# Eleven reciprocal square roots: from Ln and Exp on ScalarE to Sqrt on ScalarE and a reciprocal on VectorE

## The chip, the core and the metric

One core of a Trainium2 chip runs the whole program. The metric is the device time of one execution in microseconds (us), as the median of several runs. TensorE (PE) does the matrix products, ScalarE (ACT) the activation functions, VectorE (DVE) elementwise work, GpSimd (POOL) a few side jobs, and SyncE (SP) issues the loads.

## The reference, cut to what matters

Two transformer-like blocks run one behind the other on 512 positions of width 1024. In between and inside them stand RMS norms. Each of them needs, for every position, the reciprocal square root of a mean of squares over the features:

```python
def rms_norm(x, w):
    y = xf * lax.rsqrt(jnp.mean(xf * xf, axis=-1, keepdims=True) + EPS)
    return (y * w.astype(jnp.float32)).astype(x.dtype)

def _rmsnorm(x, g):
    y = x32 * lax.rsqrt(jnp.mean(x32 * x32, axis=-1, keepdims=True) + RMS_EPS)
    return y.astype(x.dtype) * g
```

Eleven such norms run over whole activations: at the start of the first block (528 positions, 16 meta tokens among them), ahead of its feed-forward part, at its end, ahead of and behind each of the second block's two feed-forward parts and its attention part, and for the two low-rank projections (256 and 768 features). The head norms inside the attention branches are computed by other code.

## The kernel before, in words

Activations lie transposed: features on the 128 partitions, positions in the free dimension. A norm goes like this. ScalarE squares the chunks of 128 features one by one, and VectorE adds them up into one tile (`ssq` or `ss2`). TensorE multiplies that tile with a matrix of ones (`sum_squares`, L687), so that each partition of the PSUM tile `A[0]` holds the sum for every position. ScalarE then makes the reciprocal root in SBUF (`rstd` or `rs2`) in its helper `root`: a Ln with scale 1/features and bias eps (L1219), a drain, and an Exp with scale -0.5 (L1221), which releases the semaphore `nrm_root`. VectorE waits for it in its helper `rooted`, and then multiplies the activations by the root: in `scaled` (lines L1754, L1995, L2082, L2249, L2271), in the final norm of the first block (L2069), or in `residual` (L2089, L2093), which adds the normed output to the stream. In `scaled` the product passes to ScalarE, which makes its high part (`hi_part`, L1227; with `modulate`, L1434, in between in the second block), and VectorE takes the low part (L1714). TensorE multiplies only when a chunk has both parts.

The root is as wide as the positions of its norm: 528 once, 768 four times (512 positions and 256 of context), and 512 six times. All eleven use all 128 partitions.

Every weight tile goes a similar way: SP loads it (`raw`), ScalarE makes the high part (`w_hi`, L1190), VectorE the low part (`w_lo`, L1676), and TensorE multiplies three times (`unit`, L675). Two slots are used in turn. Every engine runs its instructions in the written order; order between engines comes from counting semaphores only. ACTIVATE instructions need their function's table on ScalarE; where it isn't there, the compiler puts an ACT_TABLE_LOAD ahead, which the source doesn't show. Other functions in the program are Exp (attention, L1305, L1525, L1587), Silu (L1257, L1452), Sigmoid (L1270, L1620), Relu, Square, Copy and Identity.

Of the kernel before, what the change touches and what calls it, by code (L numbers as in the profile page):

```python
# [26 lines left out]
ACT = mybir.ActivationFunctionType  # L27
# [5 lines left out]
SEQ = 512  # L33
META = 16
T1 = META + SEQ
CTX = 256
T2 = CTX + SEQ
# [171 lines left out]
def build(nc, I, out):  # L209
    with ExitStack() as ctx:  # L210
        def sem(name):
            return ctx.enter_context(nc.semaphore(name))

        def ps(name, cols):
            return ctx.enter_context(nc.psum_tensor(name, [P, cols], F32))
# [3 lines left out]
        def at(name, off, shape, dt=F32):  # L219
            return nc.alloc_sbuf_tensor_at(name, [P] + list(shape), dt, offset=base0 + off)  # L220
# [25 lines left out]
        def cst(name, lo=0, hi=P):  # L246
            a, n = _C[name]
            return const[lo:hi, a:a + n]
# [3 lines left out]
        eps_col = cst("eps")  # L252
# [14 lines left out]
        rstd = at("rstd", SCR + 5 * 4 * T1, [T1])  # L267
# [75 lines left out]
        rs2 = at("rstd2", E + 3 * 4 * T2, [T2])  # L343
# [57 lines left out]
        A = [ps(f"aux{s}", 1024) for s in range(2)]  # L401
# [26 lines left out]
        nrm_root = sem("nrm_root")  # L428
# [33 lines left out]
        def two(ap, n):  # L462

            return ap.rearrange("p (s n) -> p s n", s=2)

        def acc(t, geo, rows=P, lo=0):

            n = geo[0][1]
            if len(geo) == 1:
                return t[lo:rows, 0:n]  # L470
            return t[:, :].rearrange("p (s n) -> p s n", s=2)[lo:rows, :, 0:n]

        def like(ap, geo):

            return ap if len(geo) == 1 else two(ap, geo[0][1])
# [704 lines left out]
        def _(act):  # L1180
# [30 lines left out]
            def root(dst, geo, features):  # L1211

                nroot[0] += 1
                act.drain()
                act.wait_ge(nrm_sum, nroot[0])
                n0 = geo[0][0]
                n1 = geo[-1][0] + geo[-1][1]
                v = dst[:, n0:n1]
                act.activation(like(v, geo), acc(A[0], geo), ACT.Ln, bias=eps_col, scale=1.0 / features)  # L1219
                act.drain()  # L1220
                act.activation(v, v, ACT.Exp, scale=-0.5).then_inc(nrm_root, 1)  # L1221

            def hi_part(dst, src):

# [12 lines left out]
            for c in range(KC):  # L1237
                act.wait_ge(xT_out, c + 1)
                square(X[:, c, :], sqb, T1)
            root(rstd, G1, D)  # L1240
            for c in range(KC):
                hi_part(HH[:, c, :], tmp[c % 2][:, :])


            with act.Fori(0, RET_H) as h:
                u = Count(U_RET, (h, 6))
                for k, dst in enumerate((rq, rk, rvT[0], rvT[1])):
                    done(u + k)
                    geo = G1 if k else GM
# [115 lines left out]
            with act.Fori(0, KC // 2) as i:  # L1365
                for e in range(2):
                    u = Count(U_CONV + 3 * e, (i, 6))
                    for k, dst in enumerate((cb, cc)):
                        s = (u + k).slot
                        done(u + k)  # L1370
                        geo = G1 if k else GM
# [8 lines left out]
            for n in range(KC):  # L1380
                u = Count(U_OUT + n)
                split(u + 2)
                act.wait_ge(evicted[u.slot], val(u.turns() + 2))
                square(X[:, n, META:T1], sqb, SEQ)
            root(rstd, GS, D)
            for c in range(KC):
                hi_part(HH[:, c, META:T1], tmp[c % 2][:, 0:SEQ])
# [20 lines left out]
            with act.Fori(0, 4) as i:  # L1408
                for e in range(2):
# [3 lines left out]
                    square_in_turn(X[:, bass.ds(i * 2 + e, 1), META:T1], sqb, SEQ, i, e)  # L1413
            nsq[0] += KC
            root(rstd, GS, D)


# [196 lines left out]
            with act.Fori(0, KC) as n:  # L1614
                u = Count(U_GATE, (n, 4))
                for k in range(2):
                    v = u + 2 * k
# [3 lines left out]
                                   bias=col_b[:, bass.ds(n + (48 + KC * k), 1)]).then_inc(evicted[v.slot], 1)  # L1621
# [49 lines left out]
        def _(dve):  # L1671
# [13 lines left out]
            def add_square(dst, buf, n, first):  # L1685

                b = buf[nsq[0] % 2][:, 0:n]
                nsq[0] += 1
                dve.drain()
                dve.wait_ge(nrm_sq, nsq[0])  # L1690
                if first:
                    dve.tensor_copy(dst, b).then_inc(nrm_add, 1)
                else:
                    dve.tensor_tensor(dst, dst, b, ALU.add).then_inc(nrm_add, 1)  # L1694
# [4 lines left out]
                dve.wait_ge(nrm_sq, val(turn(i, nsq[0] + 1 + e, 2)))  # L1699
                dve.tensor_tensor(dst, dst, buf[(nsq[0] + e) % 2][:, 0:n], ALU.add).then_inc(nrm_add, 1)  # L1700

            def rooted():

                nroot[0] += 1
                dve.drain()
                dve.wait_ge(nrm_root, nroot[0])

            def scaled(chunks, bufs, hi, lo, scale):

                n0 = nap[0]  # L1710

                def low(c):
                    dve.wait_ge(ap_hi, n0 + c + 1)
                    dve.tensor_tensor(lo(c), bufs(c), hi(c).bitcast(F32), ALU.subtract).then_inc(ap_lo, 1)  # L1714

                for c in range(chunks):
                    if c >= 2:
                        dve.drain()
                    scale(c, bufs(c)).then_inc(ap_tmp, 1)
                    if c >= 1:  # L1720
                        low(c - 1)
                low(chunks - 1)
                nap[0] += chunks
                dve.drain()
# [19 lines left out]
            for c in range(KC):  # L1744
# [3 lines left out]
                if c >= 1:  # L1748
                    add_square(ssq[:, :], sqb, T1, c == 1)
            add_square(ssq[:, :], sqb, T1, False)  # L1750
            rooted()

            scaled(KC, lambda c: tmp[c % 2][:, :], lambda c: HH[:, c, :], lambda c: HL[:, c, :],
                   lambda c, b: dve.scalar_tensor_tensor(out=b, in0=X[:, c, :], scalar=col_a[:, c:c + 1],  # L1754
# [229 lines left out]
            for n in range(KC):  # L1984
# [5 lines left out]
                if n >= 1:  # L1990
                    add_square(ssq[:, 0:SEQ], sqb, SEQ, n == 1)
            add_square(ssq[:, 0:SEQ], sqb, SEQ, False)
            rooted()
            scaled(KC, lambda c: tmp[c % 2][:, 0:SEQ], lambda c: HH[:, c, META:T1], lambda c: HL[:, c, META:T1],
                   lambda c, b: dve.scalar_tensor_tensor(out=b, in0=X[:, c, META:T1], scalar=col_a[:, 8 + c:9 + c],  # L1995
                                                         in1=rstd[:, 0:SEQ], op0=ALU.mult, op1=ALU.mult))
# [62 lines left out]
            dve.memset(ssq[:, 0:SEQ], 0.0)  # L2059
            ff_down(FF1 // D - 1, True)  # L2060
            nsq[0] += KC
            rooted()


            def by_column(ap):
# [8 lines left out]
            def sums2(n0):  # L2074
                for c in range(KC):
                    add_square(ss2[:, n0:T2], tm2, T2 - n0, c == 0)
                rooted()

            def normed(n0):

# [3 lines left out]
            def residual(i, n0):  # L2084

                for c in range(KC):
                    for e, (a, b) in enumerate(((CTX, T2), (0, CTX))):
                        if a >= n0:
                            dve.scalar_tensor_tensor(out=Y2[:, c, a:b], in0=Y2[:, c, a:b], scalar=resg[i][:, c, e:e + 1],  # L2089
                                                     in1=rs2[:, a:b], op0=ALU.mult, op1=ALU.mult)  # L2090
                    dve.drain()  # L2091
                    x = X2[:, c, n0:T2]
                    dve.tensor_tensor(x, x, Y2[:, c, n0:T2], ALU.add).then_inc(x2_out, 1)  # L2093

            sums2(0)
            normed(0)

# [51 lines left out]
            dve.wait_ge(rpb_in, 16 * GRID_H)  # L2149
            dve.wait_ge(y_zero, 1)  # L2150
            swiglu(U_FA, G2, 0, 32, False, True)
            rooted()
            residual(0, 0)
            sums2(0)
            normed(0)

# [87 lines left out]

            for k in range(2):
                add_square(ss2[:, :], tm2, T2, k == 0)
            rooted()
            scaled(2, lambda c: tm2[c % 2][:, :], lambda c: CKH[:, c, :], lambda c: CKL[:, c, :],
                   lambda c, b: dve.scalar_tensor_tensor(out=b, in0=ckvT[:, c, :], scalar=col_b[:, 70 + c:71 + c],  # L2249
                                                         in1=rs2[:, :], op0=ALU.mult, op1=ALU.mult))  # L2250
# [15 lines left out]
            rotate(mkr[R, CTX:T2], 1)  # L2266
            dve.drain()
            dve.tensor_copy(mks[0][R, :], mkr[R, :])
            rooted()
            scaled(6, lambda c: tm2[c % 2][:, 0:SEQ], lambda c: CQH[:, c, :], lambda c: CQL[:, c, :],  # L2270
                   lambda c, b: dve.scalar_tensor_tensor(out=b, in0=cqT[:, c, :], scalar=col_b[:, 64 + c:65 + c],  # L2271
                                                         in1=rs2[:, 0:SEQ], op0=ALU.mult, op1=ALU.mult))
# [67 lines left out]
            with dve.Fori(0, KC) as n:  # L2340
                u = Count(U_GATE, (n, 4))
                for k in range(2):
                    v = u + (2 * k)
# [18 lines left out]
                    split(Count(U_OUT2 + 2 + e, (i, 2)))  # L2362
                    add_in_turn(ss2[:, CTX:T2], tm2, SEQ, i, e)
            nsq[0] += KC
            rooted()
            residual(1, CTX)
            sums2(CTX)
            normed(CTX)
            dve.wait_ge(y_zero, 2)
            swiglu(U_FB, GL, CTX, 54, True, False)  # L2370
            rooted()
            residual(2, CTX)


# [32 lines left out]
```

## Time and profile before

| | |
|---|---|
| median of 3 runs | 3187.33 us (3177.83 to 3195.09) |
| profiled execution, its own time | 3191.74 us |
| span of the profile | 3190.0 us |
| TensorE / VectorE / ScalarE busy | 91% / 46% / 34% of the span |
| mean granted clock of TensorE | 0.947 of full speed |
| ACT_TABLE_LOAD at the eleven roots | 22, two for each |

Busy time is the time in which an engine executes something. Idle time of an engine matters only where TensorE in the end waits for it too.

### The profile page before, as it was taken

The page shows a single profiled execution, that of the slowest core. Times are in us where ns is not written, and L with a number is a line of the kernel's source. Part 1 is how long each engine was busy: PE and PEld are TensorE (multiplying, and loading weights), DVE is VectorE, ACT ScalarE, POOL GpSimd, SP SyncE. Part 2 cuts the span into 40 slices and gives each one's busy share as a digit, 9 for nine tenths or more (in the row PEclk, how much of TensorE's full clock was granted, in tenths as well). Part 3 has the DMA queues.
Part 4 walks back from the last instruction along what each step waited for, and adds up shares of the span by engine and source line. Part 5 has one row for each costly group of instructions (what it writes and reads, how often), then busy time and mean ns, then how long its engine had stood idle before and what let it go on. Part 6 is the DMA issues. An engine that isn't in the chain of part 4 may idle for free.

```text
span 3190.0 us, 42398 instructions
## 1 busy us (share of the span) xinstructions
PE 2903.6 (91%) x14689; PEld 2441.5 (77%) x14689; DVE 1461.0 (46%) x2270; ACT 1083.0 (34%) x1597; POOL 35.4 (1%) x27
## 2 busy tenths in 40 slices
PE   6999999899998999959999998499888899599997
PEld 4778777689876888749999998488656677378885
DVE  4335444445655666563333324654444334533335
ACT  3223455432223223253222123432433344442322
POOL 0000000000000000010000000000000000000000
PEclk9999999899999999979999999699989899799998
DMA  3224211234433555322222222001100023123332
GB/s 105 60 65 139 67 46 53 62 123 123 126 116 108 161 164 158 113 58 59 66 59 66 63 61 61 20 27 32 44 17 14 22 70 95 52 86 95 95 92 66
DMA packets 423953, 248.13 MB, mean 78 GB/s; under 512 B 15289, under 2 KB 403850, under 8 KB 423738
## 3 DMA queue, kind: packets, MB, share of 16 engines
q1 hardware_dynamic: 423866, 247.01, 26.4%
q8 instruction: 50, 0.82, 0.1%
q14 instruction: 37, 0.30, 0.0%
HBM read 244.88 MB, written 2.10 MB: 77 GB/s over the span
## 4 chain that ended last, share of the span: by engine, by line
PE 69%; issue 20%; DVE 5%; ACT 4%; DVEq 1%; ACTq 1%; DMA 0%; POOL 0%; POOLq 0%
PE unit_acc L675 62%; PE aux L1081 2%; PE aux L1105 2%; PE aux L660 1%; PE aux L994 1%; ACT w_hi L1190 1%; DVE ssq L1694 1%; PE aux L687 1%; DVE x L2093 1%; DVE mla_stat L2294 1%; ACT h_hi L1227 1%; DVE w_lo L1676 1%; PE aux L976 1%; PE aux L760 1%; DVEq L2091 0%
## 5 line engine op out<-in xcount | busy, mean ns | idle before, releaser
L675 PE MATMUL unit_acc<-h_hi,w_hi 128*128 128x512 f32 (+2 forms) x2816 | 885.5, 360 | 60.9 <-DVE h_lo L1714 39.5
L675 PE MATMUL unit_acc<-h_lo,w_hi 128*128 128x512 f32 (+2 forms) x2816 | 866.6, 354 | 0.0
L675 PE MATMUL unit_acc<-h_hi,w_lo 128*128 128x512 f32 (+2 forms) x2816 | 864.9, 353 | 0.0
L1676 DVE TENSOR_TENSOR w_lo<-raw,w_hi 128x1024 fp32r<-128x1024 f32 (+3 forms) x405 | 484.8, 1197 | 620.2 <-ACT w_hi L1190 619.3
L1190 ACT ACTIVATE w_hi<-raw 128x1024 fp32r<-128x1024 f32 (+3 forms) x405 | 419.7, 1036 | 841.2 <-PE unit_acc L675 787.0
L675 PEld LDWEIGHTS unit_acc<-h_hi,w_hi 128*128 128x128 f32 x2816 | 504.7, 191 | 153.9 <-issue 50.6
L675 PEld LDWEIGHTS unit_acc<-h_hi,w_lo 128*128 128x128 f32 x2816 | 507.3, 191 | 57.6
L675 PEld LDWEIGHTS unit_acc<-h_lo,w_hi 128*128 128x128 f32 x2816 | 508.9, 191 | 53.0
L675 PE MATMUL unit_acc<-branch_hi,w_hi 128*128 128x512 f32 x448 | 178.3, 398 | 0.0
L675 PE MATMUL unit_acc<-branch_lo,w_hi 128*128 128x512 f32 x448 | 177.5, 396 | 0.0
L675 PE MATMUL unit_acc<-branch_hi,w_lo 128*128 128x512 f32 x448 | 177.4, 396 | 0.0
L675 PE MATMUL unit_acc<-u_hi,w_hi 128*128 128x384 f32 (+1 forms) x528 | 159.2, 356 | 0.0
L675 PE MATMUL unit_acc<-u_hi,w_lo 128*128 128x384 f32 (+1 forms) x528 | 159.1, 355 | 0.0
L675 PE MATMUL unit_acc<-u_lo,w_hi 128*128 128x384 f32 (+1 forms) x528 | 159.1, 355 | 0.0
L1819 DVE SCALAR_TENSOR_TENSOR ada_sum<-ada_raw,silu_c,ada_sum 128x512 f32<-128x512 f32 x203 | 145.8, 749 | 18.6 <-issue 13.4
L2119 DVE TENSOR_TENSOR y<-unit_acc,y 128x768 f32 (+2 forms) x48 | 39.6, 825 | 175.4 <-PE unit_acc L675 175.4
L2104 DVE TENSOR_TENSOR tmp<-unit_acc,tmp 128x768 f32<-128x768 f32 (+1 forms) x44 | 36.3, 825 | 167.1 <-PE unit_acc L675 167.1
L687 PE MATMUL aux<-ssq,const 128*128 128x384 f32 (+2 forms) x32 | 22.2, 820 | 97.1 <-DVE ssq L1694 83.8
L675 PEld LDWEIGHTS unit_acc<-u_hi,w_hi 128*128 128x128 f32 x528 | 96.4, 188 | 8.3 <-DVE u_lo L2110 0.3
L675 PEld LDWEIGHTS unit_acc<-u_hi,w_lo 128*128 128x128 f32 x528 | 96.4, 188 | 8.1
L675 PEld LDWEIGHTS unit_acc<-u_lo,w_hi 128*128 128x128 f32 x528 | 96.4, 188 | 8.0
L675 PEld LDWEIGHTS unit_acc<-branch_hi,w_lo 128*128 128x128 f32 x448 | 84.3, 188 | 20.7
(282 smaller groups left out, 2989.0 us busy)
## 6 DMA issues: line engine op xcount, KB each, us to landing
raw<-in_w_in_dram SPq DMA_DIRECT2D x132, 512.0 KB, 3.9
raw<-in_ffn_w_dram SPq DMA_DIRECT2D x120, 512.0 KB, 3.8
ada_raw<-in_w_ada_dram SPq DMA_DIRECT2D x72, 512.0 KB, 4.7
raw<-in_w_up_dram SPq DMA_DIRECT2D x32, 512.0 KB, 4.3
raw<-in_w_down_dram SPq DMA_DIRECT2D x32, 512.0 KB, 3.9
raw<-in_w_branch_dram SPq DMA_DIRECT2D x24, 512.0 KB, 3.9
raw<-in_w_out_dram SPq DMA_DIRECT2D x16, 512.0 KB, 3.8
raw<-in_ffn_w_dram SPq DMA_DIRECT2D x16, 384.0 KB, 3.4
```

The lines of the kernel that those rows point to most:

```text
L660: return pe.transpose(dst, src, ident[k0:k0 + k, k0:k0 + k])
L675: last = pe.matmul(G[s][0:n, 512 * j:512 * j + m], w[s][:, k, 0:n], x[:, k, a:a + m], start=(k == 0 and i == 0), stop=(k == kc - 1 and i = ...
L687: last = pe.matmul(A[0][:, 512 * j:512 * j + m], ones, src[:, a:a + m], start=True, stop=True)
L760: last = pe.matmul(A[1][:, a:a + 1], s[:, c * P:c * P + P], ones[:, 0:1], start=True, stop=True)
L976: pe.matmul(A[0][:, b:b + 256], q, nk[r, a:a + 256], start=True, stop=True)
L1081: last = pe.matmul(A[0][:, a:a + m], mq[0:QK, P * t:P * t + P], mk[0:QK, a:a + m], start=True, stop=True)
L1105: last = pe.matmul(A[1][:, 768:768 + VD], mT[t % 2][:, j, :], mV[:, j, :], start=(j == 0), stop=(j == 5))
L1190: act.activation(wh[v.slot][:, 0:kc, :], raw[v.slot][:, 0:kc, :], ACT.Copy).then_inc(hi_split, 1)
L1676: dve.tensor_tensor(wl[s][:, 0:kc, :], raw[s][:, 0:kc, :], wh[s][:, 0:kc, :].bitcast(F32), ALU.subtract).then_inc(lo_split, 1)
L1819: last = dve.scalar_tensor_tensor(out=s[:, :], in0=w, scalar=c, in1=s[:, :], op0=ALU.mult, op1=ALU.add)
L2104: dve.tensor_tensor(like(tm2[1][:, n0:T2], geo), acc(G[s], geo), like(tm2[0][:, n0:T2], geo), ALU.mult).then_inc(evicted[s], 1)
L2119: dve.tensor_tensor(y, p, y, ALU.add).then_inc(evicted[u.slot], 1)
```

## The change

`root` makes a Sqrt in place of Ln, drain and Exp, and releases the semaphore from it. `rooted` is given the tile and its columns, takes the reciprocal of it in place on VectorE after the wait, and drains. All eleven callers of `rooted` pass the tile on.

```diff
@@ ScalarE, root(dst, geo, features)
-                act.activation(like(v, geo), acc(A[0], geo), ACT.Ln, bias=eps_col, scale=1.0 / features)
-                act.drain()
-                act.activation(v, v, ACT.Exp, scale=-0.5).then_inc(nrm_root, 1)
+                act.activation(like(v, geo), acc(A[0], geo), ACT.Sqrt, bias=eps_col,
+                               scale=1.0 / features).then_inc(nrm_root, 1)
@@ VectorE
-            def rooted():
+            def rooted(dst, n0, n1):
                 nroot[0] += 1
                 dve.drain()
                 dve.wait_ge(nrm_root, nroot[0])
+                dve.reciprocal(dst[:, n0:n1], dst[:, n0:n1])
+                dve.drain()
@@ its callers
-            rooted()
+            rooted(rstd, 0, T1)      # first norm, 528 columns
...
-            rooted()
+            rooted(rstd, 0, SEQ)     # two norms, 512 columns
...
-                rooted()
+                rooted(rs2, n0, T2)  # sums2: once 768, once 768, once 512 columns
...
-            rooted()
+            rooted(rs2, 0, T2)       # behind the first SwiGLU, and ckv: 768 columns
...
-            rooted()
+            rooted(rs2, 0, SEQ)      # cq: 512 columns
...
-            rooted()
+            rooted(rs2, CTX, T2)     # behind attention and behind the second SwiGLU: 512 columns
```

## Rows read from the trace of the kernel before

**Rows 1.** Page, parts 1 and 4: busy times; chain by engine.
```profile
PE 2903.6 (91%) x14689; PEld 2441.5 (77%) x14689; DVE 1461.0 (46%) x2270; ACT 1083.0 (34%) x1597; POOL 35.4 (1%) x27
...
PE 69%; issue 20%; DVE 5%; ACT 4%; DVEq 1%; ACTq 1%; DMA 0%; POOL 0%; POOLq 0%
```

**Rows 2.** Timeline, root of 512 columns: start, duration (us), engine, line, [idle before].
```profile
993.79 1.28 ACT L1219 ACT_TABLE_LOAD   x1
...
996.09 2.08 PE L687 MATMUL aux<-ssq,const 128*128 128x512 f32 x2 [4.03 <-DVE ssq L1694]
998.20 0.69 ACT L1219 ACTIVATE rstd<-aux,const 128x512 f32<-128x512 f32 x1 [3.12 <-PE aux L687]
998.94 1.28 ACT L1221 ACT_TABLE_LOAD   x1
1000.23 0.63 ACT L1221 ACTIVATE rstd<-rstd 128x512 f32<-128x512 f32 x1
1000.90 1.42 DVE L1995 SCALAR_TENSOR_TENSOR tmp<-x,col_a,rstd 128x512 f32<-128x512 f32 x2 [4.86 <-ACT rstd L1221]
...
1003.18 0.77 PE L675 MATMUL unit_acc<-h_hi,w_hi 128*128 128x512 f32 x1 [5.02 <-DVE h_lo L1714]
```

**Rows 3.** Timeline, a root of 768 columns.
```profile
1414.66 0.90 ACT L1219 ACTIVATE rstd<-aux,const 128x768 f32<-128x768 f32 x1 [2.81 <-PE aux L687]
1415.62 1.28 ACT L1221 ACT_TABLE_LOAD   x1
1416.91 0.84 ACT L1221 ACTIVATE rstd<-rstd 128x768 f32<-128x768 f32 x1
1417.79 1.83 DVE L2082 TENSOR_TENSOR tmp<-x,rstd 128x768 f32<-128x768 f32 x2 [6.14 <-ACT rstd L1221]
```

**Rows 4.** Timeline behind the root for ckv, up to where TensorE goes on.
```profile
2275.13 1.95 DVE L2249 SCALAR_TENSOR_TENSOR tmp<-ckv,col_b,rstd 128x768 f32<-128x768 f32 x2 [8.13 <-ACT rstd L1221]
...
2278.77 1.06 ACT L1190 ACTIVATE w_hi<-raw 128x1024 fp32r<-128x1024 f32 x1
2279.86 1.23 DVE L1676 TENSOR_TENSOR w_lo<-raw,w_hi 128x1024 fp32r<-128x1024 f32 x1 [0.91 <-ACT w_hi L1190]
...
2281.14 0.79 PE L675 MATMUL unit_acc<-h_hi,w_hi 128*128 128x512 f32 x1 [3.58 <-DVE w_lo L1676]
```

**Rows 5.** ScalarE's groups: xcount | busy us, mean ns | idle before.
```profile
L1452 ACT ACT_TABLE_LOAD x32 | 41.1, 1283 | 8.5 <-issue 5.9 <-DVE h_lo L1714 2.6
...
L1219 ACT ACT_TABLE_LOAD x11 | 14.1, 1283 | 0.7
L1221 ACT ACT_TABLE_LOAD x11 | 14.1, 1283 | 0.6
```

**Rows 6.** VectorE's groups: reciprocals, an equally small operation, and two wide ones.
```profile
L2093 DVE TENSOR_TENSOR x<-x,y 128x512 f32<-128x512 f32 x16 | 11.1, 693 | 1.2
...
L2093 DVE TENSOR_TENSOR x<-x,y 128x768 f32<-128x768 f32 x8 | 7.7, 959 | 0.6
...
L1905 DVE RECIPROCAL diff_rc<-diff_sum 128x2 f32<-128x2 f32 x32 | 5.3, 166 | 41.4 <-ACT diff_p L1305 41.4
...
L2210 DVE RECIPROCAL na_stat<-na_stat 128x1 f32<-128x1 f32 x32 | 5.3, 164 | 2.4
...
L2201 DVE TENSOR_SCALAR na_stat<-na_stat 128x1 f32<-128x1 f32 x32 | 4.9, 154 | 3.2 <-issue 0.9
...
L2302 DVE RECIPROCAL mla_stat<-mla_stat 128x1 f32<-128x1 f32 x32 | 4.9, 153 | 0.0
```

**Rows 7.** Timeline of ScalarE: first Exp of either attention of the second block.
```profile
2071.42 0.51 ACT L1525 ACTIVATE na_p<-na_p,na_stat 128x256 f32<-128x256 f32 x1 [7.75 <-DVE na_stat L2201]
...
2334.80 0.90 ACT L1587 ACTIVATE mla_p<-aux,mla_stat 128x768 f32<-128x768 f32 x1 [6.84 <-DVE mla_stat L2296]
```

**Rows 8.** Windows around a root: busy us of PE, PEld, DVE, ACT, POOL; PEclk.
```profile
991.00:1008.00 17.00, 7.95 (x18) 4.05 (x17) 10.00 (x14) 8.61 (x11) 0.00 (x0) 0.60 0.28 88
1008.00:1013.00 5.00, 3.69 (x14) 1.95 (x13) 4.22 (x7) 1.89 (x3) 0.00 (x0) 1.00 0.00 0
```

More of the change, by code:

```diff
@@ L2061, in _ @@
             nsq[0] += KC
-            rooted()
+            rooted(rstd, 0, SEQ)
             def by_column(ap):
@@ L2246, in _ @@
                 add_square(ss2[:, :], tm2, T2, k == 0)
-            rooted()
+            rooted(rs2, 0, T2)
             scaled(2, lambda c: tm2[c % 2][:, :], lambda c: CKH[:, c, :], lambda c: CKL[:, c, :],
@@ L2268, in _ @@
             dve.tensor_copy(mks[0][R, :], mkr[R, :])
-            rooted()
+            rooted(rs2, 0, SEQ)
             scaled(6, lambda c: tm2[c % 2][:, 0:SEQ], lambda c: CQH[:, c, :], lambda c: CQL[:, c, :],
@@ L2364, in _ @@
             nsq[0] += KC
-            rooted()
+            rooted(rs2, CTX, T2)
             residual(1, CTX)
@@ L2370, in _ @@
             swiglu(U_FB, GL, CTX, 54, True, False)
-            rooted()
+            rooted(rs2, CTX, T2)
             residual(2, CTX)
```

## The prediction, as it was put on record before the changed kernel ran

> **What bounds the kernel now.** I read the page first. TensorE is busy for 91% of the span and carries 69% of the chain that ended last; VectorE and ScalarE are half idle and hold 5% and 4% of it [rows 1]. So a microsecond on either of these counts only where TensorE stands still for it. The chain's stops lie at the norms, so I went to the timeline of one root. TensorE sums the squares at 996.09, then has nothing to do, and starts again at 1003.18, after 5.02 us of idleness that end with the first low part of the scaled activations [rows 2]. In between runs a strictly serial row: Ln, the load of a table, Exp, the first product on VectorE. Nothing else is ready to fill it, since every following product needs the root.
>
> The same holds at all eleven roots. VectorE waits for the Exp at each of them, 4.86 us in the one shown and 6.14 us at one of 768 columns [rows 2, 3]. At the final norm of the first block and at the three residual steps, VectorE's multiplications follow the root directly and TensorE waits for them. The root for ckv looks different, since TensorE still has projections to do, but it runs out of them: it waits 3.58 us for a low part of weights, which ScalarE could start only behind its high parts of ckv, and these stand behind the root [rows 4]. So I count all eleven fully.
>
> **What goes.** From the end of Ln to the first product on VectorE: at 512 columns Ln ends at 998.89 and the product starts at 1000.90, which is 2.01 us (a gap of 0.05, the load 1.28, Exp 0.63, semaphore 0.04) [rows 2]. At 768 columns it is 1415.56 to 1417.79, which is 2.23 us [rows 3]. I take 2.03 for the one of 528. Sum: 6 x 2.01 + 2.03 + 4 x 2.23 = 23.0 us.
>
> The Sqrt takes the place of the Ln, reads the same PSUM columns with the same scale and bias, and I give it the same 0.69 and 0.90 us.
>
> **Table loads besides.** Every root has two, 1283 ns each [rows 5]. The one ahead of Ln is free: in the timeline it starts at 993.79, directly behind ScalarE's last work, and is over before TensorE has even begun the sum at 996.09 [rows 2]. A load for Sqrt would stand there as well, just as free, or be missing where Sqrt's table is still in place (no other function between two roots than Square, Copy, Relu or Identity, if these need no table of their own). The new cost is on the other side: behind a root the table is no longer Exp's. The two attentions of the second block have no load of their own now, and would get one: one for the neighbourhood attention and one for each turn of the other's loop of three. The first Exp of each comes after ScalarE has been idle for 7.75 and 6.84 us, waiting for the row maximum [rows 7]. A load of 1.28 us fits in there, if it is placed ahead of the wait, as the one at Ln is. I book nothing; without that cover it would be 4 x 1.28 = 5.1 us. The 32 loads of Silu stay, as its loop starts with another table than it ends with in either version [rows 5].
>
> The Trainium skill ("ScalarE: Activation LUTs", section Table sets: the hidden batching unit) says that logarithm and exponential share one set, so that the pair would need one load. The trace disagrees: each of the eleven Exps has its own, between it and its Ln [rows 5]. By that page the part removed would be 11 x 1.28 = 14.1 us smaller; the rows decide.
>
> **What is added.** On VectorE, a reciprocal of n columns in place, a drain, and the semaphore from ScalarE. Semaphore: 0.04 us as now. Drain: the reciprocal at L2210 also comes behind a drain, with 2.4 us of gaps over 32, which is 0.08 us each [rows 6]. Together 11 x 0.12 = 1.3 us.
>
> Then the reciprocal itself, which decides everything. The trace has reciprocals of one or two columns only. A wide one is 0.15 us of fixed time plus n times a price per column. Bounds from the nearest rows:
> - Below: an ordinary operation costs (959 - 693) / 256 = 1.04 ns per column [rows 6]. The reciprocal of two columns takes 166 ns, and that of one column behind a drain 164: a step of 2 ns, little more than this.
> - Above: the other reciprocal of one column takes 153 ns, so that the step to 166 would be 13 ns.
> - In between: an operation of one column without a division, in the same place as the reciprocal of 164 ns, takes 154, so 153 without its column [rows 6]. The reciprocal of two columns is 13 ns above that, or 6.5 ns for each.
>
> The three rows don't agree, because the sites differ by some ns in how they start. I take 6.5 ns: both reciprocals behind a wait or a drain (164 and 166) stand 10 and 12 ns above the plain operation, which one column more at 1.04 ns can't explain, and a division that is worked out in several passes for each column would.
>
> With 6.5 ns: 0.153 + 512 x 0.0065 = 3.48 us, 3.59 for 528 and 5.15 for 768. All eleven have 6 x 512 + 528 + 4 x 768 = 6672 columns: 11 x 0.153 + 6672 x 0.0065 = 45.1 us.
>
> **Sum.** 45.1 + 1.3 - 23.0 = +23.4 us. A root of 512 columns loses 1.6 us, one of 768 loses 3.0 us. The profiled execution took 3191.74 us, so it would be 3215 us; the median of the runs shown is 4.4 us below the profiled one, and I put the forecast against it: 3187.33 + 23.4 = 3210.7 us, rounded to 3211, or 0.7% slower. The price at which the change breaks even is (23.0 - 1.3 - 1.7) / 6672 = 3.0 ns per column.
>
> TensorE's clock: around a root the granted clock averages 0.60, between the levels 1.2 and 2.4 GHz, after TensorE had waited 4.03 and 5.02 us; then it is 1.00 again [rows 2, 8]. These stops are long already, so I add nothing. At ckv the stop grows from 3.58 to 6.6 us; TensorE's 7.95 busy us in a window at 0.60 could be at best half as long at full clock, so a new slow stretch costs below 4 us.
>
> **The rivals.**
> 1. *A column a cycle.* VectorE divides at 1.04 ns per column, as the step from 164 to 166 ns suggests. Then 512 columns take 0.69 us like the addition [rows 6], all eleven 8.6 us, and the result is 8.6 + 1.3 - 23.0 = -13.1 us: 3174 us. At 2 ns per column it is -6.7 us. This is the one on the other side, and it decides below 3.0 ns. For it: the like-for-like rows. Against it: the 10 ns above the plain operation.
> 2. *Eight cycles a column.* A division of eight passes costs 8 x 1.04 = 8.3 ns per column: 57.3 us in all, +35.6 us, 3223 us. For it: it lies between the bounds of 2 and 13. Against it: two columns should then take 153 + 17 = 170 ns where the row has 166. The Trainium skill has this as a rule ("VectorE: DVE Perf Modes", section First, the fixed hardware budget: the reciprocal runs iterative divide operations with a repeat count of 8).
> 3. *The table costs more.* Loads for Exp come behind the wait and are exposed (+5.1 us), or Square, Copy, Identity or Relu behind Sqrt need a table load each time. In the trace these run behind Exp and Silu without any. It would add to whichever price holds: 3216 us with mine.
> 4. *The change doesn't shorten the wait for Exp*, because ScalarE has two tables to load ahead of Sqrt, or Sqrt is slower than Ln. The load ahead of Ln ends 3.1 us before Ln starts [rows 2], so a second would still be hidden. Little speaks for it.
>
> **Chances.** Mine (5 to 7.5 ns per column) 0.38; eight cycles 0.21; a column or two a cycle's time, up to 3 ns, 0.32; above 9 ns 0.03; between 3 and 5 ns, or the tables, 0.06. The time given is that of the likeliest, 3211 us, whose own range is 3200 to 3218. The range for 8 in 10 must hold both sides: from 3170 (rival 1 with some us of scatter) to 3228 (rival 2 with the same). What a measurement of this kernel can tell from no change is about 0.5%, or 16 us: below 3171 counts as faster, above 3203 as slower. Rival 1 lies just inside "no change". Slower: 0.36 of mine, 0.21, 0.03 and little of the rest, 0.60; no change 0.32; faster 0.08.
>
> **What would show it.** In the profile after: one ACTIVATE of 0.69 or 0.90 us at each root and no load between it and VectorE; RECIPROCAL rows of 3.5 and 5.1 us (0.69 and 0.95 if rival 1 holds, 4.4 and 6.5 if rival 2 does); TensorE's stop ahead of L675 5.02 + 1.6 = 6.6 us in place of 5.02; loads at the roots 6 in place of 22; one new load at L1525 and three at L1587, each ending before its Exp's wait does. The forecast is wrong above all if the price per column isn't near 6.5 ns; it moves by 6.7 us for every ns.

## The result: 0.85% slower, and the profile after

The changed kernel takes 3214.32 us (median of 6 runs, 3206.86 to 3224.07) against 3189.51 us for the one before (6 runs, three of them those of the table above; 3177.83 to 3195.09). The ratio is 1.0085 with a 95% interval of 1.006 to 1.0109, so 19 to 35 us more. The forecast was 23.4 us more and a time of 3211 us.

The timeline of the changed kernel at the root whose rows before are [rows 2] (start, duration, engine, line, idle before):

```profile
994.09 1.28 ACT L1219 ACT_TABLE_LOAD   x1
...
996.39 2.07 PE L687 MATMUL aux<-ssq,const 128*128 128x512 f32 x2 [4.03 <-DVE ssq L1693]
998.50 0.69 ACT L1219 ACTIVATE rstd<-aux,const 128x512 f32<-128x512 f32 x1 [3.12 <-PE aux L687]
999.22 3.35 DVE L1706 RECIPROCAL rstd<-rstd 128x512 f32<-128x512 f32 x1 [2.88 <-ACT rstd L1219]
1002.65 1.42 DVE L1996 SCALAR_TENSOR_TENSOR tmp<-x,col_a,rstd 128x512 f32<-128x512 f32 x2
...
1004.93 0.76 PE L675 MATMUL unit_acc<-h_hi,w_hi 128*128 128x512 f32 x1 [6.47 <-DVE h_lo L1715]
```

Up to the end of the activation everything stands as before. The load and the Exp behind it are gone: VectorE starts 0.03 us after the Sqrt has ended at 999.19. But it then divides for 3.35 us, and with the drain (0.08 us) the first product starts 3.46 us after the activation, where it was 2.01. TensorE's idle time ahead of L675 is 6.47 us in place of 5.02. The whole 1.45 us arrive there.

All reciprocals of the changed kernel, as groups of VectorE (xcount | busy us, mean ns | idle before):

```profile
L1706 DVE RECIPROCAL rstd<-rstd 128x512 f32<-128x512 f32 x6 | 20.1, 3353 | 13.4 <-ACT rstd L1219 13.3
L1706 DVE RECIPROCAL rstd<-rstd 128x768 f32<-128x768 f32 x4 | 19.8, 4953 | 16.2 <-ACT rstd L1219 16.2
L1906 DVE RECIPROCAL diff_rc<-diff_sum 128x2 f32<-128x2 f32 x32 | 5.3, 166 | 41.4 <-ACT diff_p L1304 41.4
L2211 DVE RECIPROCAL na_stat<-na_stat 128x1 f32<-128x1 f32 x32 | 5.3, 164 | 3.1 <-issue 0.9
L2303 DVE RECIPROCAL mla_stat<-mla_stat 128x1 f32<-128x1 f32 x32 | 4.9, 153 | 0.0
L1706 DVE RECIPROCAL rstd<-rstd 128x528 f32<-128x528 f32 x1 | 3.5, 3452 | 3.0 <-ACT rstd L1219 3.0
```

Two widths give the price: (4953 - 3353) / 256 = 6.25 ns for a column of all 128 partitions, and 3353 - 512 x 6.25 = 153 ns besides. That is six times the 1.04 ns of the addition [rows 6]. The eleven take 20.1 + 19.8 + 3.5 = 43.4 us.

The table loads, as groups of ScalarE:

```profile
L1451 ACT ACT_TABLE_LOAD x32 | 41.1, 1283 | 9.9 <-issue 7.0 <-DVE h_lo L1715 2.9
...
L1219 ACT ACT_TABLE_LOAD x6 | 7.7, 1283 | 0.4
...
L1586 ACT ACT_TABLE_LOAD x3 | 3.8, 1283 | 0.4
...
L1524 ACT ACT_TABLE_LOAD x1 | 1.3, 1283 | 0.1
```

Six at the roots in place of 22, and four new ones ahead of Exps. The timeline shows that a new one is covered:

```profile
2087.56 1.28 ACT L1524 ACT_TABLE_LOAD   x1
2093.79 0.51 ACT L1524 ACTIVATE na_p<-na_p,na_stat 128x256 f32<-128x256 f32 x1 [4.95 <-DVE na_stat L2202]
```

It ends at 2088.84, and the Exp still waits 4.95 us for the row maximum.

With the terms as measured: 43.4 + 11 x 0.11 - 23.0 = +21.6 us. The profiled execution, the longest of the six, spans 3222.3 us, 32.3 us more than before. Of the other 10.7 us, 10.4 lie in one place away from the roots. It is the longest unbroken run of products in the chain (start, duration in us), from the trace before and then from the one after:

```profile
1437.05 542.13 PE unit_acc L675 x3126
```

```profile
1442.88 552.54 PE unit_acc L675 x3126
```

The same 3126 products took 10.4 us longer, at a granted clock of 1.00 in both. 32.3 - 10.4 = 21.9 us is close to what the roots make, but not all the rest is roots: two more stretches differ and nearly cancel. From the root ahead of the second block's attention to the one for ckv the changed kernel needs 3.9 us less than its longer root would give, and from the root for cq to the one behind the attention 3.6 us more. Whether the 10.4 us belong to the change was a question for an experiment.

### The profile page after: what moved, and what is told of

It reads as the page before. It is cut to its first block, busy times and chain, and to the rows that moved or that the text cites. A ratio compares the mean times of both kernels' runs of the same rounds, so it can differ in the third digit from the quotient of the medians.

```text
span 3222.3 us, 42386 instructions
## 1 busy us (share of the span) xinstructions
PE 2912.5 (90%) x14689; PEld 2451.0 (76%) x14689; DVE 1504.2 (47%) x2281; ACT 1059.6 (33%) x1574; POOL 35.4 (1%) x27
## 4 chain that ended last, share of the span: by engine, by line
PE 69%; issue 19%; DVE 6%; ACT 3%; DVEq 1%; ACTq 1%; DMA 0%; POOL 0%; POOLq 0%
PE unit_acc L675 62%; PE aux L1081 2%; PE aux L1105 2%; DVE rstd L1706 1%; PE aux L660 1%; PE aux L994 1%; ACT w_hi L1190 1%; DVE ssq L1693 1%; PE aux L687 1%; DVE x L2094 1%; DVE mla_stat L2295 1%; ACT h_hi L1226 1%; DVE w_lo L1675 1%; PE aux L976 1%; PE aux L760 1%
## 5 line engine op out<-in xcount | busy, mean ns | idle before, releaser
L675 PE MATMUL unit_acc<-h_hi,w_hi 128*128 128x512 f32 (+2 forms) x2816 | 885.1, 360 | 76.0 <-DVE h_lo L1715 51.6
L675 PE MATMUL unit_acc<-h_lo,w_hi 128*128 128x512 f32 (+2 forms) x2816 | 866.4, 354 | 0.0
L675 PE MATMUL unit_acc<-h_hi,w_lo 128*128 128x512 f32 (+2 forms) x2816 | 864.7, 353 | 0.0
L1190 ACT ACTIVATE w_hi<-raw 128x1024 fp32r<-128x1024 f32 (+3 forms) x405 | 419.7, 1036 | 846.5 <-PE unit_acc L675 797.3
L675 PEld LDWEIGHTS unit_acc<-h_hi,w_hi 128*128 128x128 f32 x2816 | 504.1, 190 | 169.0 <-issue 60.7
L675 PEld LDWEIGHTS unit_acc<-h_hi,w_lo 128*128 128x128 f32 x2816 | 506.8, 190 | 57.2
L675 PEld LDWEIGHTS unit_acc<-h_lo,w_hi 128*128 128x128 f32 x2816 | 507.9, 190 | 52.6
L675 PE MATMUL unit_acc<-branch_hi,w_hi 128*128 128x512 f32 x448 | 178.1, 397 | 0.0
L675 PE MATMUL unit_acc<-branch_lo,w_hi 128*128 128x512 f32 x448 | 177.3, 396 | 0.0
L675 PE MATMUL unit_acc<-branch_hi,w_lo 128*128 128x512 f32 x448 | 177.2, 395 | 0.0
L675 PE MATMUL unit_acc<-u_hi,w_hi 128*128 128x384 f32 (+1 forms) x528 | 160.4, 358 | 0.0
L675 PE MATMUL unit_acc<-u_lo,w_hi 128*128 128x384 f32 (+1 forms) x528 | 160.2, 357 | 0.0
L675 PE MATMUL unit_acc<-u_hi,w_lo 128*128 128x384 f32 (+1 forms) x528 | 160.2, 357 | 0.0
L675 PEld LDWEIGHTS unit_acc<-u_hi,w_hi 128*128 128x128 f32 x528 | 96.8, 188 | 8.3 <-DVE u_lo L2111 0.3
L675 PEld LDWEIGHTS unit_acc<-u_hi,w_lo 128*128 128x128 f32 x528 | 96.8, 188 | 8.1
L675 PEld LDWEIGHTS unit_acc<-u_lo,w_hi 128*128 128x128 f32 x528 | 96.8, 188 | 8.1
L675 PEld LDWEIGHTS unit_acc<-branch_hi,w_lo 128*128 128x128 f32 x448 | 84.2, 188 | 20.7
```

What stands on the lines that cost most here:

```text
L675: last = pe.matmul(G[s][0:n, 512 * j:512 * j + m], w[s][:, k, 0:n], x[:, k, a:a + m], start=(k == 0 and i == 0), stop=(k == kc - 1 and i = ...
L1190: act.activation(wh[v.slot][:, 0:kc, :], raw[v.slot][:, 0:kc, :], ACT.Copy).then_inc(hi_split, 1)
```

## The experiments

**One activation for the whole root.** It leaves nothing but the part that goes: the changed kernel with another function and without the reciprocal.

```diff
-                act.activation(like(v, geo), acc(A[0], geo), ACT.Sqrt, bias=eps_col,
+                act.activation(like(v, geo), acc(A[0], geo), ACT.Abs_reciprocal_sqrt, bias=eps_col,
                                scale=1.0 / features).then_inc(nrm_root, 1)
...
-                dve.reciprocal(dst[:, n0:n1], dst[:, n0:n1])
-                dve.drain()
```

> One ACTIVATE of Abs_reciprocal_sqrt with scale 1/features and bias eps makes the whole root; no Exp, no Sqrt, no reciprocal. If the stretch from the end of Ln to the first product is fully on the path at all eleven roots, as the prediction counted, this is 23 us faster than before (ratio 0.993) and in its profile VectorE's product starts 0.04 us behind the activation. Rival: some of the stretch is covered by other work, or the loads for Exp behind the roots are exposed; then it gains clearly less, 10 us or so.

Measured: 3157.14 us (6 runs) against 3186.45 us for before on the same chip, ratio 0.9909, interval 0.9886 to 0.9932, so 22 to 36 us less. The 23 us of the theory are at the near end of it, the rival's 10 us outside. The timeline of its root:

```profile
991.82 0.69 ACT L1219 ACTIVATE rstd<-aux,const 128x512 f32<-128x512 f32 x1 [2.17 <-PE aux L687]
992.54 1.42 DVE L1994 SCALAR_TENSOR_TENSOR tmp<-x,col_a,rstd 128x512 f32<-128x512 f32 x2 [1.94 <-ACT rstd L1219]
...
994.83 0.76 PE L675 MATMUL unit_acc<-h_hi,w_hi 128*128 128x512 f32 x1 [3.05 <-DVE h_lo L1713]
```

The product starts 0.03 us behind the activation, and TensorE's stop is 3.05 us: 1.97 us less than the 5.02 of before, against 2.01 - 0.04 = 1.97 worked out. This kernel has the same tables as the changed one (six loads at the roots, one and three new ones ahead of the Exps), so these cost nothing that could be seen. Timed once more on another chip, it was faster again:

> The single activation once more, on the same chip as the later memsets: ratio to before 0.991 to 0.993, within the interval of its first timing.

Measured: 3153.49 us against 3193.27 us, ratio 0.9882, interval 0.9858 to 0.9905. Its 0.991 to 0.993 were too modest, the measured value lies below them and the two intervals overlap. So something more than 23 us is gained. It isn't in the stretches at the roots: these shrink by 1.98 us at 512 columns, 1.99 at 528 and 2.20 at 768, which is 22.7 us in all. Nor is it TensorE's sum of squares ahead of the root. Here that ran at full clock, 1.13 us, where the kernel before took 2.08 [rows 2]; but a second trace of the kernel before has 1.23 us at the same root, so this differs between executions.

```profile
992.14 1.13 PE L687 MATMUL aux<-ssq,const 128*128 128x512 f32 x2 [4.04 <-DVE ssq L1693]
```

```profile
992.27 1.23 PE L687 MATMUL aux<-ssq,const 128*128 128x512 f32 x2 [4.03 <-DVE ssq L1694]
```

One stretch differs more than the executions of one kernel do. These are windows from the activation at the root ahead of the second block's attention to the activation at the root for ckv (busy us of PE, PEld, DVE, ACT, POOL; PEclk): two traces of the kernel before, two of the single activation, one of the changed kernel.

```profile
2015.41:2272.00 256.59, 225.01 (x1217) 197.14 (x1218) 128.78 (x337) 85.77 (x192) 7.58 (x8) 0.90 0.11 31
2021.19:2277.86 256.67, 225.01 (x1217) 197.19 (x1218) 128.78 (x337) 85.77 (x193) 7.55 (x8) 0.90 0.11 31
```

```profile
2000.26:2249.21 248.95, 219.00 (x1217) 191.89 (x1218) 128.76 (x337) 84.95 (x191) 7.57 (x8) 0.93 0.12 32
2001.74:2251.78 250.04, 220.15 (x1217) 192.94 (x1218) 128.82 (x337) 84.90 (x192) 7.56 (x8) 0.93 0.12 32
```

```profile
2035.72:2291.26 255.54, 220.57 (x1217) 193.28 (x1218) 133.69 (x338) 84.91 (x191) 7.56 (x8) 0.93 0.12 31
```

With the single activation TensorE is busy 6.0 and 4.9 us less for the same 1217 products, at a granted clock of 0.93 in place of 0.90. A third trace of the kernel before, that of the price by width below, has 223.50 us at 0.91. Over the whole span, too, the mean granted clock was 0.954 to 0.959 in all 11 runs of the single activation and 0.945 to 0.953 in all 23 of the kernel before on the same chips. A part of that rise is only that stops at the lower level are shorter; the busy time in the windows is a gain besides. Why the clock comes out better in this stretch was not found. The reciprocals don't undo it: the changed kernel has 0.93 there as well. How much of what is left is scatter stays open. At one root the gain is even smaller than worked out: in the second timing's trace VectorE was still at other work when the root for cq was ready, and started 0.92 us behind the activation.

**The activation without a second table.** A Copy behind the same activation costs what Exp costs (0.63 us each) and has no load of its own here. The edit is on top of the single activation.

```diff
                 act.activation(like(v, geo), acc(A[0], geo), ACT.Abs_reciprocal_sqrt, bias=eps_col,
-                               scale=1.0 / features).then_inc(nrm_root, 1)
+                               scale=1.0 / features)
+                act.drain()
+                act.activation(v, v, ACT.Copy).then_inc(nrm_root, 1)
```

> As the one with a single activation, but with a drain and a Copy in place of itself behind it, which has the duration of Exp (0.63 or 0.84 us) and needs no table. Against before it lacks only the eleven loads between the two activations: 11 x 1.28 = 14.1 us faster (ratio 0.9956), and 9 us slower than the single activation. Rival: the load isn't what the stretch waits for; then it is as long as before.

Measured: 3168.66 us (7 runs), ratio 0.995, interval 0.993 to 0.9971, so 9 to 22 us less than before and 11.5 us more than the single activation. The load was on the path: the 14.1 us expected lie within the interval, whose middle is 15.9.

```profile
990.56 0.69 ACT L1219 ACTIVATE rstd<-aux,const 128x512 f32<-128x512 f32 x1 [2.17 <-PE aux L687]
991.31 0.63 ACT L1222 ACTIVATE rstd<-rstd 128x512 f32<-128x512 f32 x1
991.97 1.41 DVE L1996 SCALAR_TENSOR_TENSOR tmp<-x,col_a,rstd 128x512 f32<-128x512 f32 x2 [2.64 <-ACT rstd L1222]
```

From the activation's end to the product it is 0.72 us here, 2.01 with the load and 0.03 with nothing: of the 2.01 us, 1.29 belong to the load, the rest to Exp.

**The reciprocal on top of Ln and Exp.** The added part alone, with the tables of before.

```diff
                 act.activation(like(v, geo), acc(A[0], geo), ACT.Ln, bias=eps_col, scale=1.0 / features)
                 act.drain()
-                act.activation(v, v, ACT.Exp, scale=-0.5).then_inc(nrm_root, 1)
+                act.activation(v, v, ACT.Exp, scale=0.5).then_inc(nrm_root, 1)
...
                 dve.wait_ge(nrm_root, nroot[0])
+                dve.reciprocal(dst[:, n0:n1], dst[:, n0:n1])
+                dve.drain()
```

> Ln and Exp stay (Exp with scale +0.5 gives the root), and the wide reciprocal comes on top, with its drain; the tables are those of before. If a reciprocal of n columns costs 0.153 us and 6.25 ns per column and all of it is on the path: 43.4 + 0.9 = 44.3 us slower than before (ratio 1.0139). Rival: some of the loss of the change comes from Sqrt's tables and not from the reciprocal; then this one is below 40 us.

Measured: 3230.47 us (6 runs), ratio 1.0136, interval 1.0107 to 1.0166, so 34 to 53 us more; the middle is 43 us, against 44.3 expected. By the rows the two parts add up: the stretches shrink by 22.7 us with the single activation and grow by 44.1 here, which makes +21.4, and the changed kernel's grow by 21.6. The times are too coarse to say as much: -29 and +43 make +14 us, with the intervals -2 to +31, and the change is +19 to +35. They agree, but a third part of some us, from the tables or the clock, isn't excluded by them.

**The price by width.** The kernel before, with pairs of instructions at VectorE's start, each width twice.

```diff
+            dve.memset(sqb[0][:, :], 2.0)
+            dve.drain()
+            for n in (1, 2, 3, 4, 8, 16, 32, 64, 128, 256, 512):
+                for r in range(2):
+                    dve.reciprocal(tmp[0][:, 0:n], sqb[0][:, 0:n])
+                    dve.drain()
+                    dve.tensor_scalar(tmp[1][:, 0:n], sqb[0][:, 0:n], 2.0, None, ALU.mult)
+                    dve.drain()
             dve.memset(ada[:, :, 1], 0.0)
```

> The kernel before, with reciprocals of 1 to 512 columns and a tensor_scalar of the same width behind each, twice, at VectorE's start. If a reciprocal costs 0.153 us and 6.25 ns per column at every width: 159, 166, 172, 178, 203, 253, 353, 553, 953, 1753 and 3353 ns. Rival: narrow ones cost about a column a cycle and the higher price starts with some width, or there is a step of eight columns; then 1, 2, 3, 4 and 8 columns lie within 10 ns of each other.

The timeline of VectorE, the second of each width:

```profile
1.97 0.16 DVE L1731 RECIPROCAL tmp<-square 128x1 f32<-128x1 f32 x1
2.21 0.15 DVE L1733 TENSOR_SCALAR tmp<-square 128x1 f32<-128x1 f32 x1
...
2.93 0.17 DVE L1731 RECIPROCAL tmp<-square 128x2 f32<-128x2 f32 x1
3.17 0.17 DVE L1733 TENSOR_SCALAR tmp<-square 128x2 f32<-128x2 f32 x1
...
5.93 0.20 DVE L1731 RECIPROCAL tmp<-square 128x8 f32<-128x8 f32 x1
6.21 0.17 DVE L1733 TENSOR_SCALAR tmp<-square 128x8 f32<-128x8 f32 x1
...
8.29 0.35 DVE L1731 RECIPROCAL tmp<-square 128x32 f32<-128x32 f32 x1
8.72 0.18 DVE L1733 TENSOR_SCALAR tmp<-square 128x32 f32<-128x32 f32 x1
...
22.13 3.35 DVE L1731 RECIPROCAL tmp<-square 128x512 f32<-128x512 f32 x1
25.56 0.43 DVE L1733 TENSOR_SCALAR tmp<-square 128x512 f32<-128x512 f32 x1
```

One line from 1 to 512 columns: 0.16, 0.17, 0.20, 0.35, 3.35 us, where 0.153 + 0.00625 n gives 0.159, 0.166, 0.203, 0.353 and 3.353. There is no step and no width below which a division is cheap per column. One and two columns simply can't tell a price of 1 ns from one of 6: the tensor_scalar also goes from 0.15 to 0.17 us between these two widths, and then stays there up to 8. This kernel ran once and isn't compared in time.

**Both kernels once more.** For the 10.4 us in the run of products.

> The kernel before once more, for its trace. In the profile of the changed kernel the longest unbroken run of products (3126 of them, from the first SwiGLU's first unit on) took 552.5 us and in the one of before 542.1 us, at full granted clock in both. Theory: this is scatter between executions, which either kernel can show, and no part of the change; then this look or the next shows the other of the two lengths than its kernel's first one. Rival: the length goes with the wide reciprocals (552.5 in both kernels that have them, 542.1 in the four that haven't); then it is 542.1 here.

> The changed kernel once more, for its trace. Theory: the run of 3126 products takes 542.1 us in some executions of this kernel too, so that the span can be 10 us below the first profile's 3222.3; the roots have the rows of the first profile to within 0.05 us. Rival: 552.5 again, because of the reciprocals or of what they shift.

The same piece of the chain, in the second trace of the kernel before and then in the second trace of the changed one:

```profile
1432.47 552.54 PE unit_acc L675 x3126
```

```profile
1449.90 543.69 PE unit_acc L675 x3126
```

The kernel before has now shown both lengths, and the changed one the long one and one near the short one. So the 10.4 us are scatter between executions, and the rival, that the length goes with the reciprocals, has fallen. It can explain a good part of how widely the runs of one kernel lie apart here. The reciprocals have the durations of the first profile, but this execution had a loss of its own, 5.2 us at a copy ahead of a root (see the last section). The spans were 3199.8 and 3210.8 us: taken alone, these two traces would have given the change 11 us, and the first two gave it 32. A difference of this size can't be read from two spans.

**Later memsets.** Reading the roots, one row stood out that isn't part of the change: VectorE's first copy of squares in two norms takes 3.03 and 3.76 us. GpSimd's memsets start at the same moment. From the trace of the single activation:

```profile
1390.61 2.66 POOL L1653 MEMSET rpb_shifted<- 128x3072 f32 x1 [784.71 <-DVE x L2068]
1390.64 3.03 DVE L1691 COPY ssq<-tmp 128x768 f32<-128x768 f32 x1
```

The edit, on top of the single activation:

```diff
-            pool.wait_ge(x2_out, KC)
+            pool.wait_ge(nrm_sum, 4)
             pool.memset(rpbT[:, :, :], 0.0).then_inc(rpb_zero, 1)
...
-            pool.wait_ge(x2_out, 3 * KC)
+            pool.wait_ge(nrm_sum, 10)
             pool.memset(Y2[:, :, CTX:T2], 0.0).then_inc(y_zero, 1)
```

> The kernel with the single activation, and GpSimd's memsets (of the shifted bias, 3072 columns, and of y, 6144 and 4096) wait for the sum of squares of the next norm in place of the last chunk of x2, so that they no longer run at the same time as VectorE's copy of the first square. That copy took 3.03 us beside a memset and 0.56 alone (768 columns), and 3.76 against 0.43 (512). If the memsets lengthen it, both copies take 0.56 and 0.43 us and the kernel gains 2.5 + 3.3 = 5.8 us over the single activation, which is 29 us below before (so ratio 0.989). Rival: the copies are long for another reason, and it is as long as the single activation.

The groups of these copies in its trace:

```profile
L1691 DVE COPY ssq<-tmp 128x768 f32<-128x768 f32 x3 | 1.7, 560 | 0.4 <-ACT tmp L1202 0.2
L1691 DVE COPY ssq<-tmp 128x512 f32<-128x512 f32 x2 | 0.9, 427 | 0.2
```

All copies are at 560 and 427 ns. The stretch from root to root around each of them shrinks by 2.5 and 3.3 us against the single activation's first trace. Measured: 3149.05 us (5 runs), ratio 0.9861, interval 0.9835 to 0.9887, beside 0.9882 for the single activation on the same chip. The copies' 5.8 us are shown by the rows. In the time the difference of 4.4 us fits them, but the intervals overlap, so the time alone doesn't show it. The profiled execution even spans 8.5 us more than that of the single activation on the same chip, since its run of 3126 products took 554.07 us.

## Why the prediction was right

- **What goes, 23.0 us.** Right. Row by row: the load and Exp are gone, and the experiments with one activation and with a Copy cut the 2.01 us into 1.29 for the load and 0.7 for Exp. That all eleven roots are fully on the path was right too. TensorE's stop grew by 1.42 us at the final norm (21.83 to 23.25) and by 2.85 at the residual step behind the first SwiGLU (28.04 to 30.89). Even at ckv, where TensorE had other work, its stop grew from 3.58 to 6.41 us; 6.6 was forecast.

```profile
2303.23 0.80 PE L675 MATMUL unit_acc<-h_hi,w_hi 128*128 128x512 f32 x1 [6.41 <-DVE w_lo L1675]
```

- **The tables.** Right: six loads for Sqrt, one and three new ones for Exp, all covered. They gave nothing and took nothing, though ScalarE has 12 fewer. One sentence of the prediction goes too far: that Copy and the like run behind Exp and Silu without any load. Fifteen loads stand directly ahead of Copies (L1190 x8, L1250 x4, L1328 x3 in the kernel before). The changed kernel has the same fifteen, so nothing came of it. The rule of the Trainium skill that logarithm and exponential share one set ("ScalarE: Activation LUTs", Table sets: the hidden batching unit) was not what this chip's program did, and following it would have put 14.1 us too little on the part removed; the experiment with the Copy shows the load's cost in the time.
- **The reciprocal.** The price was 6.5 ns per column in the forecast and is 6.25, with the 153 ns of fixed time as stated; 45.1 us were forecast and 43.4 measured. The choice between the rows was right for a reason that was only half right: of the 10 ns between the reciprocal of 164 and the tensor_scalar of 154 the division explains 5, the rest is how the site starts, as the 153 of the third site shows [rows 6]. The step from 164 to 166 ns, which spoke for rival 1, came from two sites as well. So that the forecast lies within 4% of the price is in part luck: the three pairings gave 2, 6.5 and 13 ns, and the argument for the middle one was only half right. The chance of 0.38 says the same.
- **Rival 1** (a column a cycle, 3174 us) fell with the first RECIPROCAL row. **Rival 2** (eight cycles, 3223 us) overstates: by it 512 columns take 4.4 us, the row has 3.35. The Trainium skill's page behind it ("VectorE: DVE Perf Modes", First, the fixed hardware budget) names a repeat count of eight. The trace agrees with it that a division costs several times the column price of an addition, and not that it is eight times: 6.25 / 1.04 is six. **Rival 3** and **rival 4** didn't occur. TensorE's stop was 6.47 us where 6.6 was forecast.
- **The sum.** +23.4 us forecast; +21.6 by the terms as measured, +21.9 by the two profiles without the run of products (closer than it should be, since other differences of 3.9 and 3.6 us cancel in it), and 19 to 35 us by the ratio, whose middle is 27. Where the 5 us between the middle and the terms would come from was not shown, and the interval doesn't ask for it. The clock was booked at nothing, and the change shows nothing: apart from the run of products TensorE's busy time is 2902.1 us against 2903.6 before. That is a sum in which the stretch from the root ahead of the attention to ckv's has 4.4 us less and the one from cq's root to that behind the attention 3.7 more. The experiment with one activation shows that an edit of these roots can come with a better clock. The granted clock around the root was 0.60 before [rows 8], and is 0.62 now:

```profile
991.00:1009.00 18.00, 7.43 (x17) 3.60 (x15) 12.70 (x14) 6.51 (x9) 0.00 (x0) 0.62 0.27 85
```

## What to carry to other kernels

An operation that runs on a half idle engine can still be the most expensive one, if it stands in a serial chain between two stretches of the busy engine: here VectorE's busy share rose by one percentage point and TensorE waited for each microsecond of it. Before an operation is moved to a wide tile, get its price per column from two wide sizes; two sizes of one and two columns bounded it here only between 2 and 13 ns. And where a chain of two activations holds a table load between them, look for one function that does both: that gained 29 us here (40 on the second chip), where the two-engine form lost 25. How exact this function is was not measured.

## What the runs showed besides

- A copy in SBUF on VectorE and a memset on GpSimd exclude each other. The copy of 768 columns takes 0.56 us alone, 3.03 beside one memset, and in the second trace of the changed kernel it had to let two pass:

```profile
1406.08 2.66 POOL L1653 MEMSET rpb_shifted<- 128x3072 f32 x1 [795.79 <-DVE x L2070]
1406.11 8.19 DVE L1691 COPY ssq<-tmp 128x768 f32<-128x768 f32 x1
1408.67 5.22 POOL L1654 MEMSET y<- 128x6144 f32 x1
```

  It works the other way round too: where the copy comes between the two memsets, the second memset takes 5.63 us, and 5.22 where it doesn't. The additions of two tensors that run beside the second memset in the other traces keep their 0.96 us. The Trainium skill has this ("SBUF — State Buffer", section SBUF: two separate sides: the port pair shared by VectorE and GpSimd is an exclusive lock for the whole instruction); the traces agree.
- The products of 384 columns in the long run come at 542.13 / 3126 = 173 ns apiece in some executions and at 552.54 / 3126 = 177 in others, at full granted clock, and two executions lay near them (543.69 and 554.07 us). Of the ten traces five have 542.1 and three 552.5. What sets the pace wasn't found; it is worth 10 us of the span, half of what the change did.
